# A head of the step that starts sooner, norm, centring, variance and bonus in the array's four quadrants, and a router product turned round

## The reference

```python
kk = heads(k * k_k); kk = kk / jnp.maximum(jnp.sqrt(jnp.sum(kk * kk, axis=-1, keepdims=True)), 1e-12)   # norm
mu = jnp.mean(y, axis=-1, keepdims=True)                                                                # centring
var = jnp.mean(jnp.square(y - mu), axis=-1, keepdims=True)                                              # variance
bonus = jnp.sum(r_h * k_h * r_k, axis=-1, keepdims=True) * v_h                                          # bonus
```

```python
aff = jax.nn.sigmoid((hf @ w_router).astype(jnp.float32))      # (2048, 1024) @ (1024, 32)
```

## Time and profile before

| | |
|---|---|
| median of 3 runs | 4377.42 us |
| the profiled execution, its own time | 4378.55 us |
| its span in the trace | 4376.8 us |
| TensorE busy with matmuls | 4030.0 us, 92% |
| VectorE, ScalarE, GpSimd busy | 1845.2, 1331.9, 470.0 us |
| granted TensorE clock, mean | 0.964 |
| norm, centring, variance, bonus | 64, 64, 64 and 64 records of 592 to 594 ns |
| 32 steps | from 159.6 to 2847 us |
| output stage up to the last logits | from 2847 to 3143 us |

### The profile page before, as it was taken

The page is one execution under the profiler, slowest core; times in us unless marked ns, Lnnn a source line. Parts: engine busy times, 40 slices in busy tenths (PEclk is TensorE's granted clock), DMA queues, the critical chain, the costliest instruction groups (busy, mean ns, idle before and its releaser), DMA issues.

```text
span 4376.8 us, 93151 instructions
## 1 busy us (share of the span) xinstructions
PE 4030.0 (92%) x36187; PEld 2805.6 (64%) x36187; DVE 1845.2 (42%) x3765; ACT 1331.9 (30%) x2995; POOL 470.0 (11%) x519
## 2 busy tenths in 40 slices
PE   7799999999999999999999999899689999999992
PEld 4578777777777787787777787745344444444440
DVE  5345554554555555555555555422511111111115
ACT  5224333333333333333333343343201111111114
POOL 1101211110210200201201201000000000000003
PEclk9889999999999999999999999999789999999996
DMA  9611211221221221221212212233289999999999
GB/s 366 222 42 61 97 48 55 86 67 56 74 78 46 82 81 43 84 70 54 84 52 72 85 43 81 78 102 122 94 349 411 411 411 411 411 411 411 411 411 376
DMA packets 292929, 760.51 MB, mean 174 GB/s; under 512 B 16466, under 2 KB 107828, under 8 KB 292532
## 3 DMA queue, kind: packets, MB, share of 16 engines
q1 hardware_dynamic: 273876, 687.60, 42.4%
q0 software_dynamic: 11520, 41.95, 2.5%
q10 hardware_dynamic: 7136, 25.23, 1.4%
HBM read 679.19 MB, written 75.52 MB: 172 GB/s over the span
## 4 chain that ended last, share of the span: by engine, by line
PE 85%; issue 6%; DVE 3%; DMA 2%; ACT 2%; SPq 1%; POOL 0%; DVEq 0%; ACTq 0%; POOLq 0%
PE duo L1066 23%; PE bank L1426 10%; PE bank L1066 10%; PE bank L1430 5%; PE bank L1456 5%; PE bank L1296 5%; PE bank L1460 3%; PE duo L1195 2%; PE duo L1193 2%; PE duo L1172 2%; PE duo L1166 1%; PE bank L1129 1%; PE bank L1113 1%; DMA adaw<-in_w_ada_dram 1%; PE duo L1407 1%
## 5 line engine op out<-in xcount | busy, mean ns | idle before, releaser
L1066 PE MATMUL duo<-hs,w 128*128 128x256 f32 x5120 | 1143.3, 381 | 27.7 <-ACT at L1492 25.3
L1066 PEld LDWEIGHTS duo<-hs,w 128*128 128x128 f32 x5120 | 970.6, 191 | 220.6 <-issue 33.7
L1066 PE MATMUL bank<-hs,w 128*128 128x256 f32 x2048 | 462.9, 379 | 0.0
L1426 PE MATMUL bank<-W,xT 128*128 128x512 f32 x1024 | 446.3, 594 | 2.2 <-DVE xT L2487 1.5
L1066 PEld LDWEIGHTS bank<-hs,w 128*128 128x128 f32 x2048 | 389.1, 190 | 52.9
L1426 PEld LDWEIGHTS bank<-W,xT 128*128 128x128 f32 x1024 | 192.6, 191 | 233.2 <-issue 233.2
L1492 ACT ACT_TABLE_LOAD x254 | 325.9, 1283 | 11.2 <-issue 6.2
L2493 DVE TENSOR_TENSOR gsig<-bank,gsig 128x512 f32<-128x512 f32 x48 | 33.2, 692 | 675.4 <-ACT gsig L1492 675.4
L1430 PE MATMUL bank<-W,xT 128*64 128x512 f32 x1024 | 230.3, 605 | 17.4 <-issue 17.4
L828 POOL TENSOR_TENSOR Tm<-Tm,idents 128x512 f32<-128x512 f32 x32 | 40.5, 1266 | 1886.1 <-DVE Tm L2202 1886.1
L1296 PE MATMUL bank<-wo,mT 128*128 128x512 f32 x512 | 231.8, 599 | 0.0
(11 more groups left out here) (423 smaller groups left out, 6318.8 us busy)
## 6 DMA issues: line engine op xcount, KB each, us to landing
W<-in_w_expert_in_dram SPq DMA_DIRECT2D x128, 2048.0 KB, 25.6
W<-in_w_expert_out_dram SPq DMA_DIRECT2D x64, 2048.0 KB, 25.4
hs<-h_s SPq DMA_DIRECT2D x224, 512.0 KB, 4.5
w<-in_w_in_dram SPq DMA_DIRECT2D x128, 256.0 KB, 4.2
adaw<-in_w_ada_dram SPq DMA_DIRECT2D x12, 2048.0 KB, 13.3
y_s<-ysb ACTq DMA_DIRECT2D x48, 512.0 KB, 6.7
xt<-in_x_dram SPq DMA_DIRECT2D x16, 512.0 KB, 11.7
WAc<-rank_s SPq DMA_DIRECT2D x32, 256.0 KB, 3.2
```

The lines of the kernel that those rows point to most:

```text
L1066: ins = mm(place(pr, n), w[:, pr, n, k, :], hs[:, n, k, :], start=n < 4 and k == 0, stop=k == KH - 1, skip_group_check=True)
L1426: ins = mm(GU[half][:, :], xT[:, slot, kk_, :], ring_rows(parts[0])[:, k, cols], start=kk_ == 0, stop=kk_ == KT - 1)
```

## The change

Three edits.

**The head of the step.** There are two buffers `pars`, and the columns of step i+1 are copied during step i (`next_par`, in pair 3); `parQ` is copied just before it is used. VectorE's first instruction of a step is now the first sum; `rkbd` stands behind `km`. TensorE's wait for `a_ready` moves from pair 0 to pair 1, because the banks are dealt out anew: pairs 0 and 2 use (SA, SD, PJ1), pairs 1 and 3 (SB, PJ0, SC).

**Block products.** `norm_and_centred` and `variance_and_bonus` replace the four matmuls of 128 rows and 128 columns by eight of 64x64. One of each two is crossed (its blocks' results land in the other half of the partitions), so that the four matmuls of a pair lie in four different quadrants. What was crossed is read crosswise: the maximum behind norm on VectorE and the logarithm behind variance on ScalarE are now two instructions of 64 partitions each. `bonus` moves from behind pair 3 into pair 2, `gup` goes to M0, and VectorE's product `bv` moves from the step's end to behind `post`. The steps 0 and 1 have no recurrence two steps back: there norm and bonus stand alone, two quadrants each.

**The router's product.** The router's 128x32 weights are now what is loaded, each at one of four groups of 32 columns of the array, and 128 columns of h2T stream; ScalarE copies the four partial sums (128x128) out, and one more matmul with `fold` (four stacked identities of 32x32, made once on GpSimd) adds them up, after the next tile's first half.

```diff
-        TRIO = [(SA, SD, SC), (SB, PJ[0], PJ[1])]
+        TRIO = [(SA, SD, PJ[1]), (SB, PJ[0], SC)]
...
+            def blocks(bk, weights, x, crossed):
+
+                for r in range(2):
+                    o = 1 - r if crossed else r
+                    ins = mm(bk[HALF[o], :], weights[HALF[r], HALF[r]], x[HALF[r], :], start=True, stop=True)
+                return ins
+
+            def norm_and_centred(i):
...
+                if q is not None:
+                    pe.wait_ge(S["yT_summed"], q + 1)
+                    pe.sem_inc(S["pair_go"])
+                    blocks(M1, center, yT, False).then_inc(S["center_done"], 1)
+                blocks(M0, ones_bd, sq, True).then_inc(S["norm_done"], 1)
+
+            def variance_and_bonus(i):
...
+                    blocks(M0, ones_bd, sq, True).then_inc(S["var_done"], 1)
+                blocks(M1, rkbd, rk, False).then_inc(S["bonus_done"], 1)
...
                     if pr == 1:
                         pe.wait_ge(S["sg_ready"], i + 1)
+                        pe.wait_ge(S["a_ready"], i + 1)
...
                     pe.wait_ge(h_in_sem[n], i * 16 + 16)
-                    if n == 3:
-                        pe.wait_ge(S["a_ready"], i + 1)
+                    if n == 3 and prior2(i) is not None:
+                        pe.wait_ge(S["S_updated"], (i - 1) * NC)
...
                 for k in range(KT):
-                    ins = mm(SC[:, 0:NE], h2T[:, s, k, :], wr[:, k, :], start=k == 0, stop=k == KT - 1)
-                ins.then_inc(S["logit_done"], 1)
+                    j = k % 4
+                    ins = mm(SC[NE * j:NE * j + NE, 0:P], wr[:, k, :], h2T[:, s, k, :], start=k < 4, stop=k >= 4)
+                ins.then_inc(S["part_done"], 1)
+
+            def fold_logits(n, s):
...
+                pe.wait_ge(S["part_copied"], n + 1)
+                mm(SD[:, 0:NE], lp[:, s, :], fold[:, :], start=True, stop=True).then_inc(S["logit_done"], 1)
...
+                    fn(rs[HALF[0], :], M0[HALF[1], :], ACT.Ln, scale=1.0 / HD, bias=epsc[HALF[0], 1:2])
+                    fn(rs[HALF[1], :], M0[HALF[0], :], ACT.Ln, scale=1.0 / HD, bias=epsc[HALF[1], 1:2])\
+                        .then_inc(S["rs_step"], 1)
...
-                V.tensor_scalar(rn[:, :], M0[:, :], 1e-24, None, ALU.max).then_inc(S["norm_max"], 1)
+                V.tensor_scalar(rn[HALF[0], :], M0[HALF[1], :], 1e-24, None, ALU.max)
+                V.tensor_scalar(rn[HALF[1], :], M0[HALF[0], :], 1e-24, None, ALU.max).then_inc(S["norm_max"], 1)
...
+                dve.wait_ge(S["bonus_done"], i + 1)
+                dve.wait_ge(S["shifted"], i * 3 + 3)
+                V.tensor_tensor(bv[p][:, :], M1[:, :], vt[:, :], ALU.mult).then_inc(S["branch"], 1)
...
+                next_par(i + 1, 1 - p)
```

More of the change, by code:

```diff
@@ L220, in build @@
         spare = sb(p4, "spare", [P, 1792])
-        par = sb(p4, "par", [P, NQ])
+        pars = [sb(p4, f"par{x}", [P, NQ]) for x in range(2)]
         parQ = sb(p4, "parQ", [P, NQ])
@@ L298, in build @@
         wr = sb(p6, "wr", [P, KT, NE])
+        fold = sb(p6, "fold", [P, NE])
+        lp = sb(p6, "lp", [P, 2, P])
         h2T = sb(p6, "h2T", [P, 2, KT, P])
@@ L852, in _ @@
             pool.wait_ge(S["merged_out"], 16 * STEPS)
+            FOLDED = 16 * KT + 3
+            nc.gpsimd.tensor_tensor(fold[:, :], ident[:, 0:NE], ident[:, NE:2 * NE], ALU.add).then_inc(S["w_step"], 1)
+            for j in (2, 3):
+                pool.wait_ge(S["w_step"], FOLDED - 4 + j)
+                nc.gpsimd.tensor_tensor(fold[:, :], fold[:, :], ident[:, j * NE:j * NE + NE], ALU.add)\
+                    .then_inc(S["w_step"], 1)
             nc.gpsimd.iota(revg[:, :].rearrange("p (n g) -> p n g", g=NGRP), pattern=[[0, NTILE], [-1, NGRP]],
@@ L1026, in bonus @@
                     pe.wait_ge(S["rs_step"], i * 2 - 3)
-                mm(M0[:, :], rkbd[:, :], rk[:, :], start=True, stop=True).then_inc(S["bonus_done"], 1)
+                mm(M0[:, :], UP[:, 2, :], GDc[:, :], start=True, stop=True).then_inc(S["gup_done"], 1)
             def centred(q, bk=M1):
@@ L1260, in head @@
                 pair(i, 1, range(4))
-                norm(i)
-                if q is not None:
-                    centred(q)
+                norm_and_centred(i)
                 pair(i, 1, range(4, NPROD))
             def tail(i, p):
-                q = prior2(i)
                 pair(i, 2, range(2))
-                if q is not None:
-                    variance(q)
+                variance_and_bonus(i)
                 pair(i, 2, range(2, NPROD))
                 pair(i, 3)
-                bonus(i)
                 gup(i)
@@ L1603, in step @@
                 q, q2 = prior(i), prior2(i)
+                par = pars[p]
                 act.wait_ge(S["par_step"], i + 1)
@@ L1758, in _ @@
             norm2(1, 1)
-            with act.Fori(1, NTILE // 2 - 1) as h:
+            for s in range(2):
+                evac5(s, s)
+                copy_part(s, s)
+                norm2(2 + s, s)
+                copy_logits(s)
+            with act.Fori(2, NTILE // 2 - 1) as h:
                 for s in range(2):
                     evac5(h * 2 + s - 2, s)
+                    copy_part(h * 2 + s - 2, s)
+                    norm2(h * 2 + s, s)
                     copy_logits(h * 2 + s - 2)
-                    norm2(h * 2 + s, s)
             affinity(0)
@@ L2078, in step @@
                 q, q2 = prior(i), prior2(i)
[L2079 to L2087 removed]
+                par = pars[p]
                 dve.wait_ge(S["par_step"], i + 1)
[L2089 to L2092 removed]
+                begin_sums(i, 0)
                 dve.wait_ge(S["sg_ready"], i + 1)
@@ L2100, in step @@
                                 ALU.mult, ALU.add).then_inc(S["km_step"], 1)
-                begin_sums(i, 0)
+                if not first(i):
+                    dve.wait_ge(S["bonus_done"], i)
+                V.tensor_scalar(rkbd[:, :], ones_bd[:, :], par[:, Q_RK:Q_RK + 1], None, ALU.mult)\
+                    .then_inc(S["rkbd_ready"], 1)
                 dve.wait_ge(S["carry_saved"], i + 1)
@@ L2169, in step @@
                 begin_sums(i, 3)
+                if q is not None:
+                    dve.wait_ge(S["gates"], i * 2)
+                next_par(i + 1, 1 - p)
                 dve.wait_ge(S["conv_step"], i * 3 + 2)
```

100 lines of the change are left out of this document (53 added, 47 removed).

## The result

The changed kernel takes 4432.04 us (median of 5 runs, 4428.99 to 4442.61) against 4377.42 of the kernel before (five runs by then, with the same median): ratio 1.0138, 95% interval 1.0119 to 1.0158. The forecast was 4314 us. It is slower by 55 us, 1.4%, where 63 were to be won. The profiled execution has a span of 4427.2 us.

The account below looks back on a forecast made before the run. TensorE, holding 85% of the chain of waits, was taken to bound the kernel. Head 28.1, blocks 25.4 and router 10.4 sum to 63.9 us, from 4378.55 to a forecast of 4314 us; 8 in 10 range 4292 to 4345.

Parts of the forecast that it names:

- The head: Start of even steps 4 to 30: TensorE's 14 waits for ScalarE, 2.01 us each, go; 28.1 us gained.
- The blocks: Block products in each step: four quadrants run at once, 0.45 us saved a group; net 25.4 us gained.
- the slower rival: Block products: passes keep their written order, a group takes 2.54 us, the edit costs 52 us; 4392 or 4397 us; chance 4%.
- The router: Router's product in the output stage: 0.62 us saved a tile over 12 tiles, 2.9 at the end; 10.4 us gained.
- The code's layout: Rival: TensorE's issue waits, 24.7 us in odd steps, move with added instructions; 10 us either way; no chance of its own.

Follow-up runs that it names:

- the kernel before in slot 110: The kernel before with only TensorE's loop of steps placed at instruction 110 of a 256-instruction code block: 4377.95 us, 0.9994 of the kernel before.
- the one with full products: The changed kernel in slot 110 with the four full 128x128 products, one maximum and one logarithm back in place of the blocks: 4356.68 us, 0.9947.
- slot 110: The changed kernel with only TensorE's loop of steps placed at instruction 110 of a 256-instruction code block: 4315.01 us, 0.9866 of the kernel before.
- slot 165: The changed kernel with its loop placed at instruction 165 of a block, a control matching its own place: 4436.00 us, 1.0120 of the kernel before.
- slot 173: The kernel before with its loop placed at instruction 173, giving its even steps the changed kernel's block edges: 4437.41 us, 1.0131 of the kernel before.
- slot 37: The changed kernel with its loop placed at instruction 37 of a block: 4313.20 us, 0.9845 of the kernel before.
- slot 224: The changed kernel with its loop placed at instruction 224 of a block: 4381.14 us, 1.0010 of the kernel before.
- late weights: The changed kernel in slot 110, every fourth step's 1 MB weight load asked for only after the recurrence: 4288.36 us, 0.9794; the kernel before likewise: 4359.20 us, 0.9961.

## Why the prediction was wrong

- **The head: right.** The forecast was 28.1 us. No L1084 waits for ScalarE any more; up to the cut, the kernel before in slot 110 takes 1597.5 us in 29 steps, the one with full products 1567.0, so 30.5. ScalarE starts its sigmoids 0.6 us after the first L1084, and VectorE's first sum starts 4.63 us after it, where the forecast had 4.7; in step 10 no L1084 waits for it.
- **The blocks: right.** The forecast was 0.45 us a group; measured are 27.5 us in 58 groups, 0.47. All four quadrants run at once, and both row halves write one bank without waiting for each other: the four matmuls start within 0.02 us. The Trainium skill, "TensorEngine Tiling (Array Packing)", Gotcha 1: PSUM Pressure, says that different row tiles cannot access one bank at the same time; the trace does not agree. The four second passes start together behind the four first ones (1030.96 and 1031.44 above), so the slower rival was not it.
- **The router: right in the sum, in part by luck.** The forecast was 10.4 us, and the output stage is 10.3 shorter. But its tiles follow each other every 15.55 to 15.66 us instead of 16.40, 0.8 us saved a tile where the forecast had 0.62; at the stage's two ends less was saved than that leaves room for.
- **The code's layout: the step that failed.** The rival said that the waits called issue "move when eight instructions a step are added. That is 10 us either way around any of these", and the forecast said of them "nothing in the change aims at it". In the trace 70 us were won elsewhere and 122 lost here. The rival was named, but no row gives its price, 10 us either way, and it stood beside the sum of the waits in one place, 24.7 us. That sum was neither whole nor a bound. The same table of the kernel before goes on with

```profile
PE duo L1193 <- issue: 11.8, 13, 1.9
PE bank L1141 <- issue: 8.8, 12, 1.1
```

  and the five edges of a step cost 57 us there, of which the first had 34. And it said only what the present place of the edges costs: the change added 17 instructions a step, not eight, and moved all five edges by 14 to 24 records, to where they cost 138 us. The stretches at the lower clock behind them, 51 us more than before, the forecast did not count at all.
- That the place did it is shown from both sides: the changed kernel loses 121 us between slot 110 and slot 165, with the same instructions, and the kernel before loses 60 in slot 173. That the changed kernel loses twice as much at nearly the same edges is not explained. Its 4315.01 us in slot 110 is a microsecond from the forecast; so near is luck, since its runs lie between 4306.70 and 4328.93.

What the traces show of an exposed edge is a time and not a count of records. TensorE goes on 2.1 us or more after the packet has started. In the changed kernel it gets to its five edges 0.97, 1.56, 1.71, 1.51 and 1.57 us after their packets have started (medians of 29 steps), and stalls at each. In slot 110 it gets there after 1.37, 2.9, 2.2, 2.75 and 2.9 us, and stalls at the first, by 0.83 us, and by 0.25 and 0.16 us at the third and fourth. The last of these packets starts only 41 records ahead of its edge and costs nothing; one in the changed kernel starts 53 ahead and costs 0.8.

What stays open is when a block is asked for. The changed kernel's fetches start near the records 240, 350, 475 and 590, those in slot 110 near 240, 400, 476 and 626, those in slot 37 near 296, 410, 522 and 649, those in slot 224 near 200, 302, 426 and 583: they move with the edges, but not by the same distance, and I have not found the rule. So it is also open why the first edge in slot 110 is asked for so late, which it is with and without the transfers of h.

## What to carry to other kernels

Where TensorE runs small matmuls for tens of microseconds, a wait called issue that returns every 256 instructions was here the fetch of its code: count the instructions, and before a change is judged, put the loop in a fixed slot in both kernels, or time two or three slots of each. An edit of a few instructions moves all edges, so the present sum of such waits does not bound what it can cost: here 57 us at the edges became 138. Keep large transfers away from the start of such a stretch; that was worth 27 and 19 us here in one slot, and nothing that the time shows in another.

## What the runs showed of the hardware

- A loop's slot alone moved the changed kernel from 4315 to 4436 us (0.9866 and 1.0120 of the kernel before), with the same instructions.
- A block of code is a packet of 16 KB that takes 0.9 to 1.5 us; at an exposed edge TensorE goes on 2.1 to 3.1 us after its start. The holes, one a block, stand about 5.2 us apart, so one fetch in time would hide it, and it often isn't in time.
- Behind 15 us of transfers at 246 to 418 GB/s the fetch of step 11 (slot 110) started 6.3 us into the recurrence, and its edge cost 2.86 us. In each such step, of which there are seven in 29, it started 5.5 to 7.2 us in, and with late weights 3.6 to 4.7.
- The lower clock follows holes: 80.3 us were lost to it with five holes a step (up to 4.5 us), 23.9 in slot 110 (up to 3.7), and 5.1 with late weights (up to 2.0).
- From the last full matmul ahead to the next one behind it takes 1.33 us with four 64x64 products of 512 columns between them, 1.93 with two full ones; behind the four, the eight L1084 records take 0.1 us more.
